# Accumulating DMAs of weight sums moved into the first feed-forward and the second attention, one PSUM copy moved ahead of the GELU, and GpSimd making three of seven low halves there

## The chip, the core and the metric

The kernel is one program on one core of a Trainium2 chip. The metric is the device time of one execution in microseconds (us), as the median of several runs; lower is better. TensorE (PE) multiplies, VectorE (DVE), ScalarE (ACT) and GpSimd (POOL) do the rest, and DMA queues bring weights from device memory (HBM) into SBUF. SyncE (SP) only issues DMAs here. GpSimd issues the DMAs of the sums on a queue of its own.

## The reference, cut to what matters

Two transformer-like blocks run one after the other on 512 positions of width 1024, all in float32:

```python
x = first_block(x, ...)     # stick-breaking attention, pooling and gating branches,
                            # then ff = square(relu(h @ w_ff_in)) @ w_ff_out    (1024 -> 4096 -> 1024)
x = second_block(x, ...)    # differential attention with 256 context rows, a long convolution (by spectra),
                            # then conv_ffn
def conv_ffn(h, p):
    a, b = jnp.split(h @ p["ffn_w_up"], 2, axis=-1)      # 1024 -> 2 x 2816
    a = short_conv(a, p["ffn_conv_w"], p["ffn_conv_b"])  # 3 taps along the positions
    return (jax.nn.gelu(a, approximate=False) * b) @ p["ffn_w_down"]
```

The change touches the weights of `ffn_w_up` in the last line, and times at which they are prepared during the first block's feed-forward and the second block's attention.

## The kernel before, in words

Every float32 product is made of three faster ones: each operand is split into a high and a low half (`wh`, `wl` for weights), and PE adds high by high, low by high and high by low. So each 512 KB unit of weights (128 x 1024) goes through a fixed line of work. SP loads it into one of four `raw` buffers (`load`, L3124) when the low half of the unit four loads earlier has been made. ACT copies it to `wh` (L1356) when PE has used the unit four before it (`SLOTS = 4`). Then `wl = raw - wh` is made by DVE (L2043) or, if the unit is in the list `POOL_LOW`, by GpSimd (L2823). PE takes the units strictly in order, and so do the three others: each engine's program is one list, and `weights(u)` in it means "do your part of all units up to u". In the first feed-forward SP also loads, through the same ring, "mod" halves that DVE reduces (L2029, L2031).

The up-projection of the last feed-forward is cheaper than the plain one for 18 of its 22 column blocks m (m 4 to 11 are run 0, m 12 to 21 are run 1): instead of eight quarter products per m it makes seven, with weight quarters a, b, c, d and their sums ac, cd, acd, abcd. I call it the paired stage. One unit there holds two quarters and is called a duo; there are 63 (28 in run 0, 35 in run 1), each read by PE in 2 x 1.44 us. Seven duos serve two m's: position 0 of the seven holds (d, b), then (ac, abcd), (cd, a), (acd, d), (b, ac), (abcd, cd), (a, acd). For each m PE makes the products abcd(m-1), cd(m), a(m-1), acd(m), d(m), b(m-1), ac(m-1) in this order. Between them ACT and DVE patch partial results in PSUM: ACT copies cd's result aside (`keep_cd`, tile `p1c`, L1940), for which PE waits before d(m); DVE makes `gate_right(m-1)` (L2743, after `value_right`, L2738), for which PE waits before b(m-1) (`times_b`). In the same lists stand the activation of earlier m's: `centre` (ACT L1915), `up_conv` (DVE L2708), `gelu` (ACT L1920), `up_gate` (DVE L2714), `gated_high` (ACT L1926, tile `FFh`) and GpSimd's `FFl` (L3050).

The sums of weights are made in HBM by DMAs from GpSimd's queue (`sum_weights(n, step)`, n the run), 2048 KB each for run 0 and 2560 KB for run 1. Step 0 copies c twice (into ac and cd), step 1 accumulates a and d onto these, step 2 copies ac to acd, step 3 accumulates d, step 4 copies acd to abcd, step 5 accumulates b. Each step's issue waits on GpSimd until the step before has landed (semaphore `d_sum`), and SP's first load of a sum waits for all eight DMAs of its run. GpSimd's queue also loads 12 units whose halves were made ahead ("pre" units, `load_pre`, `wh<-in_wd` and `wl<-in_wd`, L2833 and L2834) and the spectral tables.

Of the kernel before, what the change touches and what calls it, by code (L numbers as in the profile page):

```python
# [165 lines left out]
DUOS = [u for u, (j, _, _) in enumerate(UNITS) if PLAN[j][0] == "sums"]  # L166
# [12 lines left out]
for _n, (_kind, _x, _) in enumerate(LOADS):  # L179
# [9 lines left out]
POOL_LOW = [u for u in range(NU) if u not in PRE and (  # L189
    u < 2 or AT["w_in_2", 0, 1536][0][0] + SLOTS - 1 <= u < AT["w_out_2", 0, 0][0][0] + SLOTS - 1  # L190
    or any(u == AT[x][0][0] for x in (((0, 1, 2), 0, 0), ((1, 1, 2), 0, 0), ("w_ff_in", 0, 0)))
    or u in DUOS and DUOS.index(u) % 7 in (2, 5))]
KT = range(8)


# [97 lines left out]
def program(nc, a):  # L293
    ctx = ExitStack()
    with ctx:
# [185 lines left out]
        def duo_ahead(f, m):  # L481
            return AT[f, m, 0][0][0] + SLOTS - 1
# [859 lines left out]
        def scalar_program(engine):  # L1342
# [176 lines left out]
            for m in range(EARLY, 8):  # L1519
                q = m - EARLY  # L1520
# [421 lines left out]
            def keep_abcd(m):  # L1942
                e.wait_ge(*PART("abcd", m))
                if m > run[0]:
                    e.wait_ge(*ADDED("c", m - 1))
                act(P5C[:, :], PS[:, BANK["up", m, 0], LEFT_HALF], ACT.Copy).then_inc(sem("part_cp"), 1)

            for first_m, count in ((0, 12), (12, 10)):
                run = RUNS[first_m > 0]
                for m in range(first_m, run[0]):  # L1950
                    weights(unit("ffn_w_up_2", 0, 2816 + m * P) + SLOTS - 1)
                    centre(m)
                    gelu(m)
                    gated_high(m, first_m)
                    for i in ((0, 1), (2, 3), (4,), ())[m]:
                        turned_high(i)
                weights(duo_ahead("cd", run[0]))
                keep_cd(run[0])
                weights(duo_ahead("d", run[0]))
                for m in run[1:]:  # L1960
                    weights(duo_ahead("abcd", m - 1))
                    keep_abcd(m - 1)
                    if m - 2 in run:
                        gelu(m - 2)
                    weights(duo_ahead("cd", m))
                    keep_cd(m)
                    if m - 2 in run:
                        gated_high(m - 2, first_m)
                    weights(duo_ahead("a", m - 1))
                    weights(duo_ahead("acd", m))  # L1970
                    weights(duo_ahead("d", m))
                    weights(duo_ahead("b", m - 1))
                    centre(m - 1)
                    weights(duo_ahead("ac", m - 1))
                m = run[-1]
                weights(duo_ahead("abcd", m))
                keep_abcd(m)
                gelu(m - 1)
                gated_high(m - 1, first_m)
                weights(unit("ffn_w_down_2", first_m * P, 0) + SLOTS - 1)  # L1980
                weights(duo_ahead("b", m))
                centre(m)
                gelu(m)
                gated_high(m, first_m)
                if first_m:
                    tables("sqrt_and_others")
                for n in range(2):
                    weights(unit("ffn_w_down_2", (first_m + count - 1) * P, n * S) + SLOTS - 1)
                    for i in range(4 if first_m else 0):
                        q = 4 * n + i  # L1990
                        if q == 7:

                            for c, s in ((0, 7), (1, 12)):
                                cols = slice(256 * c, 256 * c + 256)
                                e.wait_ge("dn_xv", 2 + c)
                                act(T(3)[:, cols], half(X, 3, 1)[:, cols], ACT.Square,
                                    accum_out=NL[:, s:s + 1]).then_inc(sem("dn_sq"), 1)
                            root(NL[:, 19:20], NL[:, 11:12], D, "nl_v", 8).then_inc(sem("nl_rt"), 1)
                            e.wait_ge("nl_v", 9)
                            e.wait_ge("fin_y", 1)  # L2000
                            act(half(Y, 3, 0), half(Y, 3, 0), ACT.Copy, scale=NL[:, 23:24]).then_inc(sem("fin_a"), 1)
                            e.wait_ge("fin_a", 1)
                            engine.dma_start(a["out"][3 * P:4 * P, 0:S], half(Y, 3, 0)).then_inc(sem("d_out"), 16)
                            continue
                        e.wait_ge(*X_READY("dn", q))
                        act(T(q % 4), half(X, i, n), ACT.Square,
                            accum_out=NL[:, 2 * i + n:2 * i + n + 1]).then_inc(sem("dn_sq"), 1)
                        if n:
                            root(NL[:, 16 + i:17 + i], NL[:, 8 + i:9 + i], D, "nl_v", 2 * i + 1).then_inc(sem("nl_rt"), 1)
# [801 lines left out]
        def gpsimd_program(engine):  # L2811
# [155 lines left out]
            for q in range(32):  # L2967
                e.wait_ge("ff_hi", q + 1)
                tt(FFl[:, q % 16, :], T(2 + q % 2), f32(FFh[:, q % 16, :]), ALU.subtract).then_inc(sem("ff_lo"), 1)  # L2969
                if q == 1:  # L2970
                    put_spectrum(0, 1)

            e.wait_ge("p_ff", 32)
            load_tables(1, 0)
            e.wait_ge("w_used", TAIL["w_ff_out"])
            load_tables(1, 1)
            for i in range(0, 8, 4):
# [20 lines left out]
                tt(x, x, T(r % 2), ALU.add).then_inc(sem("rp_add"), 1)  # L2998


            sum_weights(0, 0)
            mine = [u for u in range(PRE[2] + 1) if u > unit("w_in_2", 0, 0) and (u in POOL_LOW or u in PRE)]
            for i, u in enumerate(mine):
                weights(u)
                if i in (0, 3, 5):
                    sum_weights(0, (0, 3, 5).index(i) + 1)
            sum_weights(0, 4)
            for o in range(2):
                for f in range(4):
                    n = 4 * o + f  # L3010
                    if f < 3:
                        weights(unit("dft_f", 128, f * P, o) + SLOTS - 1)
                    for c in range(2):
                        e.wait_ge("ys_hi", 2 * n + c + 1)
                        tt(YS[n % 3][1][:, c, :], T(2 + 2 * (n % 2) + c), f32(YS[n % 3][0][:, c, :]),
                           ALU.subtract).then_inc(sem("ys_lo"), 1)
                    if f >= 2:
                        weights(unit("dft_i", 0, 0, o) + SLOTS - 1 if f == 2 else unit("dft_i", P, 0, o) + SLOTS - 1)
                weights(unit("dft_i", 3 * P, 0, o) + SLOTS - 1)
                e.wait_ge("ac_v", 4 * o + 2)  # L3020
                e.wait_ge("u_ev", 4 if o == 0 else 8)
                tt(U[:, 2, 0:512], T(4), U[:, 2, (o + 1) * S:(o + 2) * S], ALU.mult).then_inc(sem("z_p"), 1)
                if o == 0:
                    weights(unit("w_in_2", 0, 1536 + 9 * P) + SLOTS - 1)
                    weights(unit("w_in_2", 0, 1536 + 10 * P) + SLOTS - 1)
                    sum_weights(0, 5)
            sum_weights(1, 0)


            weights(unit("w_out_2", 3 * P, 0) + SLOTS - 1)  # L3030
            for q in range(6):
# [1 line left out]
                e.wait_ge("o2_v", q + 1)  # L3033
                e.wait_ge("d_xb", 16)
                tt(x, x, T(q % 4), ALU.add).then_inc(sem("o2_xp"), 1)
            sum_weights(1, 1)


            for hf in range(2):
# [23 lines left out]
            for first_m, count in ((0, 12), (12, 10)):  # L3063
                run = RUNS[first_m > 0]
                if first_m == 0:
                    shared_sums()
                    for m in range(run[0]):
                        gated_low(m, 0)
                        if m == 1:
                            sum_weights(1, 2)  # L3070
                weights(duo_ahead("d", run[0]))
                for m in run[1:]:
                    weights(duo_ahead("cd", m))
                    if m - 2 in run:
                        gated_low(m - 2, first_m)
                    weights(duo_ahead("ac", m - 1))
                    if m in (5, 7, 9):
                        sum_weights(1, 3 + (5, 7, 9).index(m))
                gated_low(run[-1] - 1, first_m)
                weights(duo_ahead("b", run[-1]))  # L3080
                gated_low(run[-1], first_m)
                for q in range(6 if first_m else 8):
                    x = half(X, q % 4, q // 4)
                    c = (8 if first_m else 0) + q
                    e.wait_ge("dn_v", c + 1)
                    e.wait_ge("n4_xn", 4)
                    e.wait_ge("o2_xv", 2)
                    e.wait_ge("dn_xp", c - 7)
                    tt(x, x, T((4 if first_m else 0) + q % 4), ALU.add).then_inc(sem("dn_xp"), 1)  # L3089
# [325 lines left out]
```

## Time and profile before

| | |
|---|---|
| median of 3 runs | 1484.92 us (1484.43 to 1485.36) |
| the profiled execution | 1485.86 us, of which the span 1484.1 us |
| mean granted clock of PE | 0.987 of full |
| busy share: PE, DVE, ACT, POOL | 97%, 59%, 44%, 26% |
| DMA | 243 MB, mean 164 GB/s |

The span goes from the first to the last recorded instruction, and all times of rows are measured from its start. Stages in the order of time: first attention to about 330 us, first feed-forward to about 765 us, second block's attention and spectral part to about 1090 us, its feed-forward with the paired stage from about 1140 us (run 0) and 1315 us (run 1). PE is nearly always busy, so the few places at which it waits are what other engines and queues cost.

### The profile page before, as it was taken

What the parts mean: (1) busy time and instruction counts of PE and PEld (TensorE: products, weight loads), DVE (VectorE), ACT (ScalarE), POOL (GpSimd) and SP (SyncE); (2) the same over time, 40 slices, a digit from 0 to 9 for tenths busy, and PEclk for the clock granted to TensorE, in tenths of its full rate; (3) what the DMA queues carried; (4) which work ended last, traced back from release to release, by engine and by line L of the source; (5) the groups of instructions that cost most, each with busy time, mean ns of one, the idle gap of its engine ahead of it and who ended that gap; (6) DMA issues with size and microseconds to landing.
All of it is one profiled execution on the core that took longest, in us unless ns stands there. A gap on an engine that the chain in (4) does not pass through costs nothing.

```text
span 1484.1 us, 19430 instructions
## 1 busy us (share of the span) xinstructions
PE 1439.5 (97%) x7644; PEld 1215.6 (82%) x7644; DVE 876.9 (59%) x1319; ACT 656.9 (44%) x1048; POOL 380.7 (26%) x317
## 2 busy tenths in 40 slices
PE   9999999999999999999999999997999897999998
PEld 7777778888888888888888888886898896889987
DVE  6456665533666543654376367786568575347854
ACT  6545763223544322343363256553445453135542
POOL 1363220111032100220033312154435331133312
PEclk9999999999999999999999999998999898999999
DMA  8351117545265453556345374566785785335541
GB/s 271 113 176 48 58 56 264 170 149 184 85 214 182 143 170 128 173 177 207 128 139 195 129 210 147 151 219 207 276 188 202 218 250 171 110 111 163 173 140 57
DMA packets 72740, 243.15 MB, mean 164 GB/s; under 512 B 8455, under 2 KB 9384, under 8 KB 67658
## 3 DMA queue, kind: packets, MB, share of 16 engines
q1 hardware_dynamic: 61274, 181.22, 36.7%
q0 software_dynamic: 9744, 55.05, 13.2%
q10 hardware_dynamic: 1632, 5.64, 1.0%
q8 instruction: 61, 1.00, 0.3%
q14 instruction: 29, 0.24, 0.0%
HBM read 229.28 MB, written 50.35 MB: 188 GB/s over the span
## 4 chain that ended last, share of the span: by engine, by line
PE 82%; DVE 6%; DMA 5%; ACT 4%; issue 2%; POOL 1%; SPq 0%; ACTq 0%; DVEq 0%; POOLq 0%
PE PS L536 79%; PE PS L549 3%; DMA raw<-sums 2%; ACT wh L1356 2%; DVE TMP L2708 2%; DVE wl L2043 2%; DMA wl<-in_wd 1%; DMA raw<-in_up 1%; POOL wl L2823 1%; DVE TMP L2091 0%; POOL X L3089 0%; ACT th L1934 0%; ACT HTh L1378 0%; ACT p1c L1940 0%; DVE HTl L2059 0%
## 5 line engine op out<-in xcount | busy, mean ns | idle before, releaser
L2043 DVE TENSOR_TENSOR wl<-raw,wh 128x1024 fp32r<-128x1024 f32 x220 | 302.0, 1377 | 314.9 <-ACT wh L1356 314.6
L1356 ACT ACTIVATE wh<-raw 128x1024 fp32r<-128x1024 f32 x255 | 266.9, 1054 | 252.7 <-PE PS L536 223.8
L536 PE MATMUL PS<-HTh,wh 128*128 128x512 f32 (+1 forms) x944 | 347.9, 370 | 3.5 <-POOL wl L2823 2.5
L536 PE MATMUL PS<-HTl,wh 128*128 128x512 f32 (+1 forms) x944 | 345.0, 367 | 0.0
L536 PE MATMUL PS<-HTh,wl 128*128 128x512 f32 (+1 forms) x944 | 340.8, 367 | 0.0
L536 PEld LDWEIGHTS PS<-HTh,wh 128*128 128x128 f32 x944 | 178.6, 189 | 38.6 <-issue 10.9
L536 PEld LDWEIGHTS PS<-HTl,wh 128*128 128x128 f32 x944 | 178.6, 189 | 27.1 <-DVE HTl L2059 0.7
L536 PEld LDWEIGHTS PS<-HTh,wl 128*128 128x128 f32 x944 | 176.4, 189 | 29.4 <-DVE wl L2043 0.2
L536 PE MATMUL PS<-wl,FFh 128*128 128x512 f32 (+1 forms) x442 | 169.9, 384 | 0.0
L536 PE MATMUL PS<-wh,FFh 128*128 128x512 f32 (+1 forms) x442 | 169.9, 384 | 0.0
L536 PE MATMUL PS<-wh,FFl 128*128 128x512 f32 (+1 forms) x442 | 169.8, 384 | 0.0
L2823 POOL TENSOR_TENSOR wl<-raw,wh 128x1024 fp32r<-128x1024 f32 x35 | 88.9, 2543 | 180.8 <-ACT wh L1356 159.9
L536 PE MATMUL PS<-th,wh 128*128 128x256 f32 x360 | 106.5, 296 | 22.0 <-ACT p1c L1940 19.4
L536 PE MATMUL PS<-th,wl 128*128 128x256 f32 x360 | 105.4, 293 | 0.0
L536 PE MATMUL PS<-tl,wh 128*128 128x256 f32 x360 | 105.3, 292 | 0.0
L2969 POOL TENSOR_TENSOR FFl<-TMP,FFh 128x512 fp32r<-128x512 f32 x32 | 43.4, 1357 | 219.5 <-ACT FFh L1591 219.5
L536 PEld LDWEIGHTS PS<-wh,FFl 128*128 128x128 f32 x442 | 83.1, 188 | 16.6
L536 PEld LDWEIGHTS PS<-wl,FFh 128*128 128x128 f32 x442 | 83.1, 188 | 16.3
L536 PEld LDWEIGHTS PS<-wh,FFh 128*128 128x128 f32 x442 | 83.1, 188 | 16.3
L536 PEld LDWEIGHTS PS<-th,wh 128*128 128x128 f32 x360 | 72.6, 202 | 24.0 <-ACT p1c L1940 21.1
L536 PEld LDWEIGHTS PS<-tl,wh 128*128 128x128 f32 x360 | 72.8, 202 | 0.1
L536 PEld LDWEIGHTS PS<-th,wl 128*128 128x128 f32 x360 | 72.6, 202 | 0.0
(359 smaller groups left out, 2344.6 us busy)
## 6 DMA issues: line engine op xcount, KB each, us to landing
raw<-in_ws SPq DMA_DIRECT2D x232, 512.0 KB, 4.2
raw<-sums SPq DMA_DIRECT2D x72, 256.0 KB, 3.5
sums<-in_up POOLq DMA_DIRECT2D x6, 2560.0 KB, 19.4
raw<-in_up SPq DMA_DIRECT2D x54, 256.0 KB, 3.6
sums<-in_up POOLq DMA_DIRECT2D x6, 2048.0 KB, 16.9
sums<-sums POOLq DMA_DIRECT2D x2, 2560.0 KB, 12.7
taps<-TMP SPq DMA_DIRECT2D x16, 256.0 KB, 2.4
tab<-in_spec POOLq DMA_DIRECT2D x8, 512.0 KB, 5.7
```

The source lines that it names most:

```text
L536: return nc.tensor.matmul(out, l, r, start=start, stop=stop, skip_group_check=True)
L549: return nc.tensor.transpose(out, in_, IDENT)
L1356: act(WH[u % SLOTS][:, :n], RAW[i % RAWS][:, :n], ACT.Copy).then_inc(sem("w_hi"), 1)
L2043: tt(WL[k][:, :n], RAW[RAW_AT["unit", u, 0] % RAWS][:, :n], f32(WH[k][:, :n]), ALU.subtract).then_inc(sem("lo_dve"), 1)
L2708: stt(z[:, do], ps[:, di], pp("ffn_conv_w_2", 22 * w + m), z[:, do], ALU.mult, ALU.add).then_inc(sem("uc_v"), 1)
L2823: tt(WL[k][:, :n], RAW[RAW_AT["unit", u, 0] % RAWS][:, :n], f32(WH[k][:, :n]), ALU.subtract).then_inc(sem("lo_pool"), 1)
L2969: tt(FFl[:, q % 16, :], T(2 + q % 2), f32(FFh[:, q % 16, :]), ALU.subtract).then_inc(sem("ff_lo"), 1)
```

## The change

There are three parts. First, all twelve steps of sums move. Run 0's steps 0 to 3 stood in the second block's attention and go to the middle of the first feed-forward's first half (after GpSimd's piece q = 15, where GpSimd has no other work for 89 us), steps 4 and 5 into its second half. Run 1's steps stood between the second block's out-projection and the paired stage of run 0; step 0 goes to where run 0's step 0 was, 1 to 4 between the units of the attention, and 5 to the end of the spectral part. No step is left in the paired stage. Second, ACT's `keep_cd(m)` goes ahead of `gelu(m-2)`. Third, GpSimd makes the low halves at positions 1, 3 and 5 of each seven duos, where it made those at 2 and 5, but none in the first four duos of each run.

```diff
@@ POOL_LOW @@
-    or u in DUOS and DUOS.index(u) % 7 in (2, 5))]
+    or u in DUOS and DUOS.index(u) % 7 in (1, 3, 5) and u not in DUOS[:4] + DUOS[28:32])]
@@ scalar_program @@
                     keep_abcd(m - 1)
+                    weights(duo_ahead("cd", m))
+                    keep_cd(m)
                     if m - 2 in run:
                         gelu(m - 2)
-                    weights(duo_ahead("cd", m))
-                    keep_cd(m)
@@ gpsimd_program @@
                 if q == 1:
                     put_spectrum(0, 1)
+                if q == 15:
+                    for step in range(4):
+                        sum_weights(0, step)
 
             e.wait_ge("p_ff", 32)
             load_tables(1, 0)
+            sum_weights(0, 4)
+            sum_weights(0, 5)
             e.wait_ge("w_used", TAIL["w_ff_out"])
             load_tables(1, 1)
...
-            sum_weights(0, 0)
+            sum_weights(1, 0)
             mine = [u for u in range(PRE[2] + 1) if u > unit("w_in_2", 0, 0) and (u in POOL_LOW or u in PRE)]
             for i, u in enumerate(mine):
                 weights(u)
-                if i in (0, 3, 5):
-                    sum_weights(0, (0, 3, 5).index(i) + 1)
-            sum_weights(0, 4)
+                if i in (0, 3, 4, 6):
+                    sum_weights(1, (0, 3, 4, 6).index(i) + 1)
...
                     weights(unit("w_in_2", 0, 1536 + 10 * P) + SLOTS - 1)
-                    sum_weights(0, 5)
-            sum_weights(1, 0)
+            sum_weights(1, 5)
...
                 tt(x, x, T(q % 4), ALU.add).then_inc(sem("o2_xp"), 1)
-            sum_weights(1, 1)
...
                         gated_low(m, 0)
-                        if m == 1:
-                            sum_weights(1, 2)
...
                     weights(duo_ahead("ac", m - 1))
-                    if m in (5, 7, 9):
-                        sum_weights(1, 3 + (5, 7, 9).index(m))
```

GpSimd's list in the first feed-forward (`FFl` is the low half of the activation, made from `FFh`; `sums<-in_up` is a copy or an accumulation):

```order
-L2969 TENSOR_TENSOR FFl_79<-TMP_145,FFh_78 128x512 x30
+L2969 TENSOR_TENSOR FFl_79<-TMP_145,FFh_78 128x512 x14
+L2844 DMA sums<-in_up 256x2048 x2
+L2846 DMA sums<-in_up 256x2048
+L2847 DMA sums<-in_up 256x2048
+L2849 DMA sums<-sums 256x2048
+L2851 DMA sums<-in_up 256x2048
+L2969 TENSOR_TENSOR FFl_79<-TMP_145,FFh_78 128x512 x16
```

Six DMAs now stand between the two halves of the `FFl` pieces, with GpSimd's waits for three landings among them.

DVE's list in the paired stage, one group of seven duos (`wl` are low halves; the removed ones go to GpSimd, the added one comes from it):

```order
-L2043 TENSOR_TENSOR wl_76<-raw_68,wh_72 128x1024
 L2732 TENSOR_TENSOR PS<-PS,p1c_140 128x256
 L2714 TENSOR_TENSOR TMP_145<-TMP_145,PS 128x512
+L2043 TENSOR_TENSOR wl_77<-raw_69,wh_73 128x1024
 L2738 TENSOR_TENSOR PS<-PS,p1c_140 128x256
 L2743 TENSOR_TENSOR PS<-p5c_141,PS 128x256
 L2724 TENSOR_TENSOR p1c_139<-PS,p1c_139 128x256
-L2043 TENSOR_TENSOR wl_74<-raw_66,wh_70 128x1024
 L2043 TENSOR_TENSOR wl_75<-raw_67,wh_71 128x1024
```

DVE loses the low halves of positions 1 and 3 and gains that of position 2, and the gained one stands between `up_gate` (L2714) and `value_right` and `gate_right` (L2738, L2743).

ACT's list in the paired stage, the same place:

```order
-L1920 ACTIVATE TMP_145<-TMP_145 128x512
 L1940 ACTIVATE p1c_139<-PS 128x256
-L1926 ACTIVATE FFh_78<-TMP_145 128x512
-L1356 ACTIVATE wh_73<-raw_69 128x1024
-L1356 ACTIVATE wh_70<-raw_66 128x1024
...
+L1920 ACTIVATE TMP_145<-TMP_145 128x512
+L1926 ACTIVATE FFh_78<-TMP_145 128x512
+L1356 ACTIVATE wh_73<-raw_69 128x1024
+L1356 ACTIVATE wh_70<-raw_66 128x1024
```

The copy `p1c` (L1940) is now ahead of the GELU (L1920). `wh_73`, the high half for position 2, stays behind `FFh` (L1926).

## Rows read from the trace of the kernel before

**Rows 1.** The page: the chain of waits by line.

```profile
PE PS L536 79%; PE PS L549 3%; DMA raw<-sums 2%; ACT wh L1356 2%; DVE TMP L2708 2%; DVE wl L2043 2%; DMA wl<-in_wd 1%; DMA raw<-in_up 1%; POOL wl L2823 1%; DVE TMP L2091 0%; POOL X L3089 0%; ACT th L1934 0%; ACT HTh L1378 0%; ACT p1c L1940 0%; DVE HTl L2059 0%
```

**Rows 2.** Timeline of PE: start, us, instruction, [idle before it <-what ended it].

```profile
1032.30 0.80 PE L536 MATMUL PS<-EDh,wh 128*128 128x512 f32 x1 [8.92 <-DMA wl<-in_wd]
...
1146.91 0.39 PE L536 MATMUL PS<-th,wh 128*128 128x256 f32 x1 [2.92 <-ACT p1c L1940]
...
1177.17 0.39 PE L536 MATMUL PS<-th,wh 128*128 128x256 f32 x1 [2.61 <-DVE wl L2043]
...
1183.12 0.58 PE L536 MATMUL PS<-th,wh 128*128 128x256 f32 x1 [3.87 <-ACT p1c L1940]
...
1207.59 0.39 PE L536 MATMUL PS<-th,wh 128*128 128x256 f32 x1 [1.69 <-ACT p1c L1940]
...
1236.91 0.58 PE L536 MATMUL PS<-th,wh 128*128 128x256 f32 x1 [8.91 <-ACT p1c L1940]
...
1323.53 0.36 PE L536 MATMUL PS<-HTh,wh 128*128 128x256 f32 x1 [2.50 <-POOL wl L2823]
...
1370.94 0.38 PE L536 MATMUL PS<-th,wh 128*128 128x256 f32 x1 [0.59 <-ACT p1c L1940]
```

**Rows 3.** Windows: length, busy us of PE, PEld, DVE, ACT, POOL, then PEclk, DMA, GB/s.

```profile
1032.00:1038.00 6.00, 5.70 (x13) 4.51 (x14) 0.17 (x1) 1.06 (x1) 0.00 (x0) 0.50 0.33 122
...
1183.00:1187.00 4.00, 3.88 (x18) 3.88 (x19) 2.48 (x3) 2.17 (x4) 4.00 (x2) 0.50 0.11 20
...
1236.00:1242.00 6.00, 5.09 (x24) 5.09 (x25) 3.99 (x6) 3.39 (x5) 4.61 (x2) 0.50 0.27 84
1324.00:1328.00 4.00, 4.00 (x25) 4.00 (x24) 0.18 (x1) 1.43 (x2) 2.37 (x1) 0.63 0.84 255
```

**Rows 4.** The chain in order of time, its waits for DMAs: issue, us to landing.

```profile
1010.96 21.30 DMA wl<-in_wd
...
1157.34 17.44 DMA raw<-in_up
...
1213.46 16.72 DMA raw<-sums
```

**Rows 5.** Timeline of POOL: the issues of sums near these waits.

```profile
1009.83 0.98 POOL L2855 DMA_DIRECT2D sums<-in_up  x1
...
1211.92 0.90 POOL L2855 DMA_DIRECT2D sums<-in_up  x1
```

**Rows 6.** DMA from 1103 to 1113 us: packets, MB, share of 16 engines.

```profile
q0 software_dynamic: 202, 1.65, 82.3%
q1 hardware_dynamic: 203, 0.77, 20.6%
```

**Rows 7.** Timeline of POOL at the start of run 1.

```profile
1314.06 6.04 POOL L3089 TENSOR_TENSOR X<-X,TMP 128x512 f32<-128x512 f32 x4 [26.59 <-DVE TMP L2798]
```

**Rows 8.** Timeline of DVE, then ACT, then PE in one period of run 1.

```profile
1353.43 1.98 DVE L2043 TENSOR_TENSOR wl<-raw,wh 128x1024 fp32r<-128x1024 f32 x1
...
1357.78 1.22 DVE L2043 TENSOR_TENSOR wl<-raw,wh 128x1024 fp32r<-128x1024 f32 x1
...
1360.31 0.43 DVE L2743 TENSOR_TENSOR PS<-p5c,PS 128x256 f32<-128x256 f32 x1
...
1359.96 0.63 ACT L1926 ACTIVATE FFh<-TMP 128x512 fp32r<-128x512 f32 x1 [1.16 <-DVE TMP L2714]
1360.50 1.99 ACT L1356 ACTIVATE wh<-raw 128x1024 fp32r<-128x1024 f32 x2
...
1361.55 0.28 PE L536 MATMUL PS<-th,wh 128*128 128x256 f32 x1
```

**Rows 9.** DMA from 504 to 593 us: the loads, KB each, median us to landing.

```profile
raw<-in_ws SPq DMA_DIRECT2D x25, 512.0 KB, 4.1
```

**Rows 10.** DMA from 869 to 872 us: the pair of accumulations of run 0.

```profile
sums<-in_up POOLq DMA_DIRECT2D x2, 2048.0 KB, 23.0
```

**Rows 11.** Timeline of ACT, a unit in the first feed-forward.

```profile
526.60 1.06 ACT L1356 ACTIVATE wh<-raw 128x1024 fp32r<-128x1024 f32 x1 [4.38 <-PE PS L536]
```

## The prediction

> **What bounds the kernel now.** I read the page first. PE is busy for 97% of the span, and the chain of waits runs through its matmuls [rows 1]; what is left on it are loads (raw<-sums 2%, wl<-in_wd 1%, raw<-in_up 1%) and pieces of ACT, DVE and GpSimd. So the time is PE's work plus the moments at which PE stands still, and I listed these in PE's timeline [rows 2]: 8.92 us at 1032, 2.92 at 1147, four waits of 2.61, 3.87, 1.69 and 8.91 in run 0, 2.50 at the start of run 1, and in run 1 a small one for `p1c` in each period of 21 us (the row of 0.59 stands for four: 0.22, 0.59, 0.59 and 0.60). Then I read the granted clock behind them, since PE runs on at half its clock after a long wait (level 1.2 instead of 2.4 GHz): 0.50 over the 6 us behind the wait at 1032, over 4 us behind the one at 1183, over 6 us from 1236, and 0.63 over 4 us from 1324 [rows 3]. The shortest wait behind which these rows show a fall is the one of 2.50.
>
> Third, why PE waits. The chain names the transfers: wl<-in_wd 21.30 us from issue to landing, raw<-in_up 17.44, raw<-sums 16.72 [rows 4]. GpSimd's timeline shows a sum issued just before: at 1009.83, a us ahead of the slow wl<-in_wd, and at 1211.92, 1.5 us ahead of the slow raw<-sums [rows 5]. While a sum accumulates, both queues move as many packets (202 and 203 in 10 us) but the sum 1.65 MB and the raw loads 0.77 MB [rows 6]: a load stream gets 77 GB/s, 6.8 us for 512 KB. The late raw holds ACT, and ACT's list holds `p1c`, which is why the rows name `p1c`.
>
> **The change part by part.** Work is neither added nor removed: the same twelve DMAs, the same low halves, the same copies. Only places move.
>
> A. Step 5 of run 0 leaves the spectral part before the pre units. The wait of 8.92 goes, and the half clock behind it, half of 6 us: 3.0. Gain 11.9. Run 1's step 5 comes about 40 us later in GpSimd's list, behind the last pre unit, where the pair of copies of run 1 stood; nothing of weights is late there in the trace before. The earlier steps of run 1 are a quarter larger than run 0's at the same places, where PE had no wait longer than 0.1 us, so I cost them at nothing; without the cover that unit loads have there, a sum of 19 us would cost what step 5 did.
>
> B. No sum runs during run 0. The four waits go, 17.1 us, and the half clock, 3.0 behind 1236 and 2.5 behind 1183 (over 2.0, which the window alone shows). Gain 22.6.
>
> C. The first low half on GpSimd in run 1 goes to DVE. GpSimd is in the additions to X for 6.04 us until 1320.1 before it begins [rows 7], and the wait of 2.50 follows; DVE's list has it before its share of the same out-projection. With the clock (0.37 of 4 us, 1.5) gain 4.0. The same edit in run 0 puts a low half of 1.22 us before `up_gate(3)` on DVE, ahead of the wait of 2.92: I take a loss of 0.5, between 0 and 1.2.
>
> D. `p1c` before the GELU. ACT no longer waits for DVE's `up_conv` before it copies, so the small waits go, 0.59 three times and 0.22: gain 2.0.
>
> E. Three of seven. Fewer low halves on DVE would relieve it, but DVE is not what PE waits for in this stage. What counts is where the added one stands. The order shows `wl_77` (position 2) between `up_gate` and `value_right`, `gate_right`, and PE waits for `gate_right` before b. In the period from 1350 [rows 8]: `gate_right` ran 1360.31 to 1360.74, PE began b at 1361.55, 0.8 us of slack. Now DVE first needs `wh` of position 2, which ACT makes behind `FFh`: `FFh` ended at 1360.5. The removed low half (1357.78, 1.22 us) lets `up_gate` and so `FFh` come earlier by 0 to 1.2 us; I take 0.6. Then wh is ready about 1360.9 (each of the two copies takes 1.0), the low half takes 1.22 alone and 1.98 beside a GpSimd operation; I take 1.3, as `FFl` is nearly over by then: 1362.2. `value_right` and `gate_right` together 0.9: 1363.1, against 1361.55. PE waits 1.5 us, where before it did not; the bounds are 0.8 (1.2 earlier, 1.22) and 2.8 (0 earlier, 1.98). It occurs once in each group of seven, except the first of each run: 3 times in run 0, 4 in run 1, 7 x 1.5 = 10.5 loss, bounds 6 and 20. This is shorter than the waits behind which the clock fell, so I add nothing for it.
>
> The rows show that GpSimd slows a DVE low half (1.22 to 1.98 us). The Trainium skill says the same of the two engines in "GPSIMD Engine Reference", section "1. Specifications": they share access to SBUF and contend when instructions have two SBUF inputs. By that rule three GpSimd lows instead of two would cost DVE up to 0.8 us once more per group, on an engine that is busy for 59%; it changes the sum only where it lengthens the low half in E.
>
> F. Steps 0 to 3 of run 0 under the first feed-forward, from 504 us. There are 25 loads in 89 us [rows 9], one per 3.56 us. Under accumulation a load takes 6.8. The pair took 23.0 us each at the median [rows 10], I take 28 until the second lands: 4.1 loads done instead of 7.9, 13.5 us short. The single one, 16 us: 2.4 instead of 4.5, 7.6 short. The copies let about as much through as is wanted; I take 3 us. Together 24 us late. The cover: `wh` is made every 4.38 + 1.06 = 5.44 us, each time when PE frees a slot [rows 11], so a low half is ready 3 x 5.44 less 2.3 = 14 us before PE needs it. A raw is asked for four loads ahead: 14.2 us at the mean interval, 21.8 where all four are units; less 2.3 and the 4.1 of the load 8 to 15 us. Cover 22 to 29 against 24: thin, yet two of the terms come from stretches in which loads had to wait for nothing else. The mod halves of the ring can be late without any loss. I take 0, and 3 to 12 us if it does not hold. GpSimd is back at about 504 + 13 + 28 + 11 + 16 = 572 (the other steps' times by the same view as [rows 10]), before 593. Steps 4 and 5 meet a lighter stretch: nothing.
>
> The rule behind the packet counts stands in the Trainium skill, "DMA: Bandwidth & Descriptors", section "Queues, rings and completion order": a DMA engine alternates between its rings packet by packet. The trace agrees (202 to 203). It speaks against this move, since larger packets of the sums take the larger part wherever they run; that is rival 2.
>
> Sum: 11.9 + 22.6 + 4.0 + 2.0 - 0.5 - 10.5 = 29.5 us off the span of 1484.1: 1454.6. The profiled execution took 1485.86, 1.8 more than its span, and the median of the runs is 1484.92, 0.8 more than the span. On that scale: 1455.4, rounded to 1455.
>
> **The rivals.**
> 1. The new wait for `gate_right` does not come, or is under 0.3 us, because PE is itself later or `FFh` earlier than I take it. For it: 0.8 us of slack today. Against it: the order of DVE's list and `wh` behind `FFh`. Time: the sum without the 10.5, 1445, or 1447 with 0.3 in each group. Chance 0.22.
> 2. The first feed-forward starves: PE waits 3 to 12 us about 545 to 590, with some 2 us of half clock. For it: the cover of F is no larger than the lateness at its lower bound. Time 1458 to 1468. Chance 0.25.
> 3. Run 0's waits stay in part, being ACT's list and not the DMAs: 1207.59 and 1177.17 remain and grow. Against it: run 1, with the same lists and no sum, has only 0.59. Time 1465 to 1475. Chance 0.04.
> 4. Slower than before: the feed-forward starves for good, since GpSimd, waiting for landings, is not back for `FFl` at 593 and the loads run at a still lower share. This decides from 30 us of waiting in the first feed-forward, thus when loads get under half of the 77 GB/s. Nothing in the rows is near that. Time 1487 to 1500. Chance 0.02.
> The forecast itself (E there, F hidden) has 0.45, with a range of its own of 1450 to 1460; 0.02 is left for what I do not see.
>
> **How the numbers follow.** The range takes the forecast's bounds (E 6 to 20: 1450 to 1465), most of rival 1 above 1443 and the smaller half of rival 2: 1443 to 1466 holds about 0.45 + 0.18 + 0.19 = 0.82. A measurement of this kernel tells about 0.2% (3 us) from no change. Faster by more: all but rival 4 and half of what is left, 0.96; same 0.01; slower 0.03.
>
> **What would show it.** At about 1010 to 1030 wl<-in_wd lands within 7 us and PE has no wait at the place of 1032. In run 0 PE has none over 3 us behind its start, raw loads take 3 to 5 us. In the paired stage PE's waits name DVE L2743, about 1.5 us each, seven of them, and none names `p1c` in run 1. At the start of run 1 no POOL wl. In the feed-forward from 504 raw loads take 8 to 16 us and ACT's wh waits for raw, but PE does not. The prediction is wrong if PE waits for wh or wl between 540 and 593, if L2743 never ends a wait of PE, or if sums of 2560 KB in the attention hold up a unit there.

## The result and the profile after

The changed kernel takes 1459.37 us at the median of four runs (1456.29 to 1461.92), against 1484.79 us for the kernel before (1484.43 to 1485.36, four runs): a ratio of 0.9828, 95% interval 0.9804 to 0.9851, so 25.4 us faster. The prediction was 1455 (1443 to 1466). The profiled execution took 1457.4 us with a span of 1455.7 us, 28.4 us less than the span before; the forecast span was 1454.6.

The page of the changed kernel: busy time by engine, then the chain of waits by line, which answers to [rows 1].

```profile
PE 1429.8 (98%) x7644; PEld 1206.5 (83%) x7644; DVE 855.4 (59%) x1314; ACT 657.1 (45%) x1048; POOL 386.1 (27%) x322
...
PE PS L536 83%; DMA raw<-in_ws 3%; PE PS L549 3%; DVE wl L2043 2%; ACT wh L1356 1%; DVE TMP L2708 1%; DVE TMP L2714 1%; DVE TMP L2091 0%; ACT th L1934 0%; ACT TMP L1920 0%; DVE PS L2743 0%; ACT HTh L1378 0%; DVE HTl L2059 0%; DVE tl L2718 0%; ACT p1c L1940 0%
```

The loads raw<-sums, wl<-in_wd and raw<-in_up have left the chain, and raw<-in_ws, the ordinary weight loads, have come onto it. The timeline of PE shows where it still stands; these rows answer to [rows 2].

```profile
569.90 0.50 PE L536 MATMUL PS<-wh,FFh 128*128 128x512 f32 x1 [0.59 <-DVE wl L2043]
...
587.92 0.47 PE L536 MATMUL PS<-HTh,wh 128*128 128x512 f32 x1 [1.41 <-DVE wl L2043]
...
1137.25 0.58 PE L536 MATMUL PS<-th,wh 128*128 128x256 f32 x1 [3.28 <-ACT p1c L1940]
...
1159.99 0.38 PE L536 MATMUL PS<-th,wh 128*128 128x256 f32 x1 [1.33 <-DVE PS L2743]
...
1375.88 0.39 PE L536 MATMUL PS<-th,wh 128*128 128x256 f32 x1 [1.32 <-DVE PS L2743]
```

The last two rows are the first and the last of seven (1160.0, 1181.7, 1203.5, 1310.7, 1332.4, 1354.2, 1375.9). Nothing is left at the place of 1032, none of the four waits of run 0, none at the start of run 1, and none for `p1c` but the one at the start of run 0. New are the seven waits for `gate_right` and two in the first feed-forward. The waits of PE that differ add up to 33.4 us before (8.92, 2.92, 2.61, 3.87, 1.69, 8.91, 2.50 and 2.00 for `p1c` in run 1) and 14.6 us after (0.59, 1.41, 3.28 and 9.3): 18.8 of the 28.4 us. The rest is the clock. In windows of 2 us, PE's busy time times the part of the clock that was missing adds up to about 12.6 us before (3.0 behind 1032, 7.9 in run 0, 1.7 behind 1324) and 2.8 us after. Two of the windows after (they answer to [rows 3]):

```profile
1137.00:1143.00 6.00, 5.75 (x27) 5.75 (x28) 3.22 (x3) 1.48 (x3) 0.57 (x1) 0.52 0.65 194
1159.00:1163.00 4.00, 3.01 (x25) 3.02 (x26) 1.22 (x4) 1.28 (x2) 2.36 (x1) 1.00 0.50 162
```

Only the wait of 3.28 us is followed by the lower level (0.52 over 6 us). Behind 1.33 us of waiting the granted clock stayed at 1.00, and so it did behind the two waits of the first feed-forward. Before, [rows 3] show four such stretches, and a fifth lay behind 1147 (0.57 over 4 us).

Why PE waits for `gate_right` is seen in one period, first DVE, then ACT, then PE; it answers to [rows 8].

```profile
1349.47 0.69 DVE L2714 TENSOR_TENSOR TMP<-TMP,PS 128x512 f32<-128x512 f32 x1 [1.12 <-ACT TMP L1920]
1351.81 1.48 DVE L2043 TENSOR_TENSOR wl<-raw,wh 128x1024 fp32r<-128x1024 f32 x1 [1.65 <-ACT wh L1356]
1353.21 0.42 DVE L2738 TENSOR_TENSOR PS<-PS,p1c 128x256 f32<-128x256 f32 x1
1353.66 0.43 DVE L2743 TENSOR_TENSOR PS<-p5c,PS 128x256 f32<-128x256 f32 x1
...
1350.20 0.63 ACT L1926 ACTIVATE FFh<-TMP 128x512 fp32r<-128x512 f32 x1 [0.75 <-DVE TMP L2714]
1350.73 1.99 ACT L1356 ACTIVATE wh<-raw 128x1024 fp32r<-128x1024 f32 x2
...
1354.15 0.38 PE L536 MATMUL PS<-th,wh 128*128 128x256 f32 x1 [1.33 <-DVE PS L2743]
```

DVE ends `up_gate` at 1350.2 and stands idle for 1.65 us, since its next work is the low half of position 2 and ACT makes that high half only behind `FFh`. Then come the low half (1.48), `value_right` and `gate_right`, and PE goes on when the last is done.

### The profile page after: what moved, and what is told of

The parts are those of the page before. It is cut to its first block, busy times and chain, and to the rows that moved or that the text cites. A ratio compares the mean times of both kernels' runs of the same rounds, so it can differ in the third digit from the quotient of the medians.

```text
span 1455.7 us, 19430 instructions
## 1 busy us (share of the span) xinstructions
PE 1429.8 (98%) x7644; PEld 1206.5 (83%) x7644; DVE 855.4 (59%) x1314; ACT 657.1 (45%) x1048; POOL 386.1 (27%) x322
## 4 chain that ended last, share of the span: by engine, by line
PE 86%; DVE 6%; ACT 3%; DMA 3%; issue 1%; POOL 0%; ACTq 0%; DVEq 0%; POOLq 0%
PE PS L536 83%; DMA raw<-in_ws 3%; PE PS L549 3%; DVE wl L2043 2%; ACT wh L1356 1%; DVE TMP L2708 1%; DVE TMP L2714 1%; DVE TMP L2091 0%; ACT th L1934 0%; ACT TMP L1920 0%; DVE PS L2743 0%; ACT HTh L1378 0%; DVE HTl L2059 0%; DVE tl L2718 0%; ACT p1c L1940 0%
## 5 line engine op out<-in xcount | busy, mean ns | idle before, releaser
L2043 DVE TENSOR_TENSOR wl<-raw,wh 128x1024 fp32r<-128x1024 f32 x215 | 280.5, 1309 | 325.9 <-ACT wh L1356 325.6
L2823 POOL TENSOR_TENSOR wl<-raw,wh 128x1024 fp32r<-128x1024 f32 x40 | 101.3, 2536 | 191.3 <-ACT wh L1356 170.4
L536 PE MATMUL PS<-th,wh 128*128 128x256 f32 x360 | 103.3, 287 | 12.6 <-DVE PS L2743 9.3
L536 PE MATMUL PS<-th,wl 128*128 128x256 f32 x360 | 102.4, 284 | 0.0
L536 PEld LDWEIGHTS PS<-th,wh 128*128 128x128 f32 x360 | 69.5, 193 | 14.3 <-DVE PS L2743 10.7
L536 PEld LDWEIGHTS PS<-tl,wh 128*128 128x128 f32 x360 | 69.6, 193 | 0.1
L536 PEld LDWEIGHTS PS<-th,wl 128*128 128x128 f32 x360 | 69.6, 193 | 0.0
```

What stands on the lines that cost most here:

```text
L536: return nc.tensor.matmul(out, l, r, start=start, stop=stop, skip_group_check=True)
L2043: tt(WL[k][:, :n], RAW[RAW_AT["unit", u, 0] % RAWS][:, :n], f32(WH[k][:, :n]), ALU.subtract).then_inc(sem("lo_dve"), 1)
L2823: tt(WL[k][:, :n], RAW[RAW_AT["unit", u, 0] % RAWS][:, :n], f32(WH[k][:, :n]), ALU.subtract).then_inc(sem("lo_pool"), 1)
```

## The experiments

Ten kernels ran, in three batches on two chips, each batch beside its own runs of the kernel before (medians 1483.70, 1484.65 and 1484.35 us); the changed kernel's own runs are those of the section on the result. I compare ratios; 0.001 of a ratio is 1.5 us. All of them keep the whole computation.

| kernel | median us (range) | ratio to before, 95% interval |
|---|---|---|
| changed kernel | 1459.37 (1456.29 to 1461.92) | 0.9828, 0.9804 to 0.9851 |
| e1: changed, `gate_right` first | 1448.15 (1442.18 to 1449.29) | 0.9751, 0.9733 to 0.9770 |
| e2: changed, positions 2 and 5 | 1451.40 (1447.40 to 1456.06) | 0.9782, 0.9762 to 0.9801 |
| e3: before, sums moved | 1456.01 (1452.22 to 1458.29) | 0.9810, 0.9794 to 0.9825 |
| e4: before, positions 1, 3, 5 | 1485.24 (1483.95 to 1486.40) | 1.0008, 0.9999 to 1.0017 |
| e5: before, copy ahead of GELU | 1473.75 (1471.78 to 1475.65) | 0.9929, 0.9917 to 0.9942 |
| e6: changed, run 0's sums in the first attention | 1454.35 (1453.16 to 1454.69) | 0.9800, 0.9786 to 0.9813 |
| e7: e6 and e1 | 1443.49 (1442.04 to 1444.32) | 0.9723, 0.9710 to 0.9737 |
| e8: e6, positions 2 and 5 but for one duo | 1443.27 (1442.65 to 1444.27) | 0.9722, 0.9708 to 0.9735 |
| e9: before, step 5 of run 0 later | 1477.14 (1474.79 to 1478.32) | 0.9950, 0.9937 to 0.9962 |
| e10: changed, sums in shorter packets | 1454.71 (1453.82 to 1455.29) | 0.9798, 0.9784 to 0.9812 |

### e1: is it the place of the low half in DVE's list?

```diff
-                    weights(duo_ahead("cd", m))
-                    weights(duo_ahead("a", m - 1))
                     value_right(m - 1)
                     gate_right(m - 1)
+                    weights(duo_ahead("cd", m))
+                    weights(duo_ahead("a", m - 1))
```

> The changed kernel with one edit in DVE's list: value_right and gate_right ahead of the low halves of weights(cd, m) and weights(a, m-1). Theory: the seven waits of 1.33 us for DVE L2743 come from the low half of position 2 standing ahead of gate_right, so they go and the time falls by about 9 us against the changed kernel (1459 to about 1450, or 1447 where the first feed-forward is as in the profiled run). Rival: DVE is short of time in this stage, so the wait only moves to a low half (PE waits for DVE wl L2043 or L2724's product) and the time stays within 3 us of the changed kernel.

Measured: 0.9751 against 0.9828, about 11 us faster than the changed kernel, where I expected 9. In PE's timeline all seven waits for L2743 are gone and no wait over 0.3 us has come in their place; behind the start of run 0 PE does not wait at all. The theory holds, the rival (DVE short of time) falls. Why it is 11 us and not 9 is said under E below. The first feed-forward was worse in the profiled run of this kernel than in the changed one's, where that part of the program is the same. Its timeline of PE there:

```profile
554.48 0.50 PE L536 MATMUL PS<-wh,FFh 128*128 128x512 f32 x1 [1.33 <-DVE wl L2043]
...
568.34 0.75 PE L536 MATMUL PS<-wh,FFh 128*128 128x512 f32 x1 [2.68 <-DVE wl L2043]
...
773.62 0.47 PE L536 MATMUL PS<-wh,tab 128*128 128x512 f32 x1 [0.37 <-issue]
```

and the window behind the second wait:

```profile
568.00:574.00 6.00, 5.67 (x18) 4.56 (x19) 2.65 (x4) 1.06 (x1) 0.00 (x0) 0.72 1.04 236
```

The matmul that the third row shows, the first with the spectral tables, is a marker behind the first feed-forward: it began at 767.8 in the kernel before, 769.8 in the changed one, here at 773.6. So this stage cost 2.0 us in the one and 5.8 in the other, and the clock went down with the wait of 2.68 (0.72 over 6 us).

### e2: GpSimd's positions as before

```diff
-    or u in DUOS and DUOS.index(u) % 7 in (1, 3, 5) and u not in DUOS[:4] + DUOS[28:32])]
+    or u in DUOS and DUOS.index(u) % 7 in (2, 5))]
```

> The changed kernel with GpSimd's positions as before the change (2 and 5, with no exception for the first four duos). Theory: the seven waits for L2743 go (9.3 us), the wait for GpSimd's low half at the start of run 1 comes back with its slow clock (2.5 + 1.5 us), run 0 starts 0.4 us sooner: about 5 us faster than the changed kernel, 1454. Rival: three of seven relieves DVE and is worth something, so that this is not faster than the changed kernel.

Measured: 0.9782 against 0.9828, 7 us faster than the changed kernel, with intervals that do not overlap. The profile has no wait for L2743, and the one at the start of run 1 is back (2.51 us for POOL wl L2823), as is the 2.93 instead of 3.28 us at the start of run 0. The theory's rows are all there. The first feed-forward has waits of 2.78 and 0.74 us, and the marker stands at 771.84. Three of seven is a loss in the changed kernel as its list of DVE stands.

### e3: the sums alone

The edit is the gpsimd part of the change's diff, made to the kernel before.

> The kernel before with only the sums moved as in the change (positions 2 and 5, GELU ahead of the copy). Theory: the sums alone carry the gain: 34.5 us of waits and slow clock less 2 to 5 us in the first feed-forward, so 1452 to 1456, as fast as or faster than the whole change. Rival: part of run 0's waits came from ACT's list, so it is 5 us or more slower than the theory says and PE still waits for p1c in run 0 by more than 1 us a period.

Measured: 0.9810, 28 us faster than before, the whole gain of the change and 2.7 us more at the median (the intervals overlap). In run 0 PE waits for `p1c` by 0.22, 0.60 and 0.63 us, as in run 1. The first feed-forward, with the same sums in it, has no wait over 0.3 us in this profiled run, and the marker stands at 767.60. So the sums carry the change.

### e4 and e5: the two other parts alone

e4 is the change's line of `POOL_LOW` in the kernel before.

> The kernel before with only GpSimd's positions changed (1, 3 and 5, none in the first four duos of a run). Theory: this part costs by itself: up to seven waits of about 1.3 us for DVE L2743 (those of run 0 may hide in its waits for sums), less 4.0 us for the wait at 1323 and its slow clock: 0 to 5 us slower than the kernel before. Rival: three of seven is worth something by itself, the time falls by 4 us or more.

Measured: 1.0008, no difference that the runs can tell. PE waits for DVE L2743 once in run 0 and three times in run 1 (1.52 to 1.54 us each; two more are under 0.3 us), two long waits of run 0 are shorter (7.42 for 8.91, 2.94 for 3.87), and the wait of 2.50 at the start of run 1 is gone. The forecast of 0 to 5 us slower holds at its lower end.

e5 has the change's edit of ACT's list alone.

> The kernel before with only the copy p1c ahead of the GELU. Theory: the four waits of 0.22 to 0.60 us in run 1 go, 2.0 us, and run 0's long waits stay, since raw loads come late there: 1 to 3 us faster than before. Rival: run 0's waits come from the GELU ahead of the copy, so that 1183 and 1236 go too, 15 us or more.

Measured: 0.9929, 10.5 us faster, where I expected 1 to 3. That theory falls in its number. The timeline of PE in run 0, to be held against [rows 2]:

```profile
1175.84 0.39 PE L536 MATMUL PS<-th,wh 128*128 128x256 f32 x1 [1.56 <-DVE wl L2043]
...
1182.10 0.39 PE L536 MATMUL PS<-th,wh 128*128 128x256 f32 x1 [2.72 <-DVE PS L2743]
...
1204.96 0.47 PE L536 MATMUL PS<-th,wh 128*128 128x256 f32 x1 [2.46 <-DVE PS L2743]
...
1226.11 0.39 PE L536 MATMUL PS<-th,wh 128*128 128x256 f32 x1 [2.12 <-DVE wl L2043]
...
1232.37 0.57 PE L536 MATMUL PS<-th,wh 128*128 128x256 f32 x1 [2.72 <-DVE PS L2743]
```

and the windows behind two of them:

```profile
1182.00:1186.00 4.00, 3.90 (x32) 3.91 (x33) 3.16 (x5) 3.12 (x4) 1.82 (x2) 1.00 0.71 228
...
1232.00:1238.00 6.00, 5.63 (x34) 5.63 (x35) 4.97 (x9) 3.63 (x5) 1.29 (x1) 0.72 0.52 175
```

The raw loads are nearly as late as before (ACT waits 7.42 and 7.99 us for them, before 8.84 and 8.59), but the waits add up to 11.6 instead of 17.1 us, and the clock stays up behind 1182 (1.00 against 0.50) and is 0.72 instead of 0.50 behind 1232. It is lower in one place: 0.57 over the 4 us from 1205, where it was 1.00 behind 1207 before. In windows of 2 us the missing clock of run 0 adds up to 4.6 us against 7.9. So there are 5.5 us of waiting, 2.0 us in run 1 and 3.3 us of clock, 10.8 against the 10.2 between the profiled spans (1484.1 and 1473.9). A late load of run 0 had cost twice: once as itself, and again because ACT, late by it, still waited for DVE's `up_conv` ahead of the copy for which PE waited. ACT's timeline in the kernel before:

```profile
1181.22 0.63 ACT L1920 ACTIVATE TMP<-TMP 128x512 f32<-128x512 f32 x1 [3.48 <-DVE TMP L2708]
```

Rival 3 of the prediction has this much truth in it.

The parts do not add: 28 and 10.5 alone, less 1 for the positions, against 25.4 together. Two things make up the 12 us. The copy's new place was good for late loads that moving the sums takes away: of its 10.5 us about 4 are left (25.4, and 7 more that e2 gives back, less 28). And the positions cost 7 us where PE has no other waits (e2), but 1 in the kernel before, where they shorten the long waits of run 0.

### e9: is step 5 the cause of the wait at 1032?

```diff
                     weights(unit("w_in_2", 0, 1536 + 10 * P) + SLOTS - 1)
-                    sum_weights(0, 5)
+            sum_weights(0, 5)
             sum_weights(1, 0)
```

> The kernel before with run 0's step 5 alone behind the last pre unit of the spectral part, just ahead of run 1's step 0. Theory: wl<-in_wd lands within 7 us, PE's wait of 8.92 us at 1032 and the slow clock behind it go, 11 to 12 us faster than before, with run 0's waits where they were. Rival: the wait at 1032 is DVE's and ACT's chain to ysl and only shows a late transfer, so less than 4 us is won.

Measured: 0.9950, 7.5 us faster; the profiled span is 11.0 us shorter (1473.1). The wait of 8.92 us is gone with its slow clock, which refutes the rival. Run 0's waits are there as expected, of other sizes (3.68 at its start, then 1.30, 4.25, 1.78 and 7.74 us). The timeline of PE shows a new one behind the new place, where the pair of copies of run 1 now follows step 5:

```profile
1065.06 0.50 PE L536 MATMUL PS<-wh,O3h 128*128 128x512 f32 x1 [2.57 <-DVE wl L2043]
```

DVE's low half ahead of it took 5.17 us, where in the kernels before and after it takes 2.25 and 2.24 beside the same additions of GpSimd (X, L3035), and these two have no wait over 0.3 us there. GpSimd's first four additions took 5.03 us here against 6.05 there, and the low half ended 1.1 us behind the last of them: GpSimd went through at its own pace and DVE gave way, where in the other two kernels both were slowed. What decides between the two stays open. That the medians show 3.5 us less than the profiles is a matter of which run was profiled: this one is the fastest of its five, 2.4 us below their median, and the one of the kernel before (1485.86) lies 1.2 us above the median here.

### e6: run 0's sums where the queues are idle

```diff
+            sum_weights(0, 0)
             keep_scores(0)
...
                 if p + 2 < PAIRS:
                     keep_scores(p + 2)
+                if p in (0, 5, 8, 11):
+                    sum_weights(0, 1 + (0, 5, 8, 11).index(p))
...
                 tt(BC[m][:, S:], EG[3 * m + 1], EG[3 * m + 2], ALU.add).then_inc(sem("eg_add"), 1)
+            sum_weights(0, 5)
...
-                if q == 15:
-                    for step in range(4):
-                        sum_weights(0, step)
...
-            sum_weights(0, 4)
-            sum_weights(0, 5)
```

> The changed kernel with run 0's six steps in the first attention (from 117 us, where the DMA engines are busy for 17%) and none in the first feed-forward. Theory: the two waits of PE at 570 and 588 (0.59 and 1.41 us in the profiled run) and the spread of the changed kernel's runs (1456 to 1462) come from raw loads under the sums of the first feed-forward; both go, 2 us against the profiled run and 2 to 5 against the median, about 1455, runs within 1 us of each other. Rival: the spread has another source, then the runs still differ by 4 to 5 us and the median falls by at most 2 us.

Measured: 0.9800 against 0.9828, 4 us faster than the changed kernel (the intervals overlap by 0.0009), and the runs lie within 1.5 us of each other instead of 5.6. The marker is back at 767.62, and no wait over 0.3 us stands in the first feed-forward; of its sum issues on GpSimd only steps 4 and 5 waited, 5.1 us each, in a place where GpSimd has nothing urgent. The two waits came from the sums under the feed-forward, and with them, as far as four runs of each can tell, the spread.

### e10: by packets?

```diff
-max_dma_last_dim=8192
+max_dma_last_dim=4096
```

(in all seven lines of `sum_weights` that start a DMA)

> The changed kernel with the sums' DMAs cut at half the length (max_dma_last_dim 4096 instead of 8192). Theory: queues alternate by packets, so packets of 4 KB on both sides give raw loads half of the rate instead of a third: loads under accumulation take 4 to 5.5 us each, PE's waits in the first feed-forward shrink below 1 us, the runs differ less, and the sums take a quarter or more longer: 1 to 4 us faster than the changed kernel. Rival: the share is not by packets (or the accumulation itself is the limit), so raw loads stay as slow, the sums only take longer, and the time stays or rises.

The views of DMA while the pair of accumulations runs, 538 to 553 us, in the changed kernel:

```profile
q0 software_dynamic: 328, 2.52, 80.7%
q1 hardware_dynamic: 335, 1.22, 21.8%
```

and the same stretch with shorter packets:

```profile
q0 software_dynamic: 537, 2.13, 71.1%
q1 hardware_dynamic: 512, 1.90, 33.8%
```

In both the two queues move nearly the same number of packets; with packets half as long the raw loads get 1.90 MB instead of 1.22 in 15 us (127 against 81 GB/s). The pair of accumulations takes GpSimd's wait from 29.8 to 32.4 us, and no wait of PE over 0.3 us is left in the first feed-forward. The time is 0.9798, 4.5 us faster than the changed kernel (the intervals overlap by 0.0008), with runs within 1.5 us, just as when the sums are elsewhere. The theory holds but for the price: the accumulations took 9% longer, not a quarter or more. By the rule of the Trainium skill that the prediction weighed ("DMA: Bandwidth & Descriptors", "Queues, rings and completion order") this is what alternation by packets would give, and the counts of both kernels agree with it.

### e7 and e8: both cures together

e7 is e6 with e1's edit. e8 is e6 with this line:

```diff
+    or u in DUOS and DUOS.index(u) % 7 in (2, 5) and u != DUOS[30])]
```

> The changed kernel with both edits that helped it: run 0's sums in the first attention and gate_right ahead of the low halves in DVE's list. Theory: they add, 1454.35 less 9.3 us: 1445, with runs within 1.5 us of each other, PE's only wait over 0.5 us in the paired stage being the one of 3.3 us at the start of run 0. Rival: one edit hides the other's gain, 1448 or more.

> The changed kernel with run 0's sums in the first attention, and GpSimd at positions 2 and 5 as before the change, but for the one duo at the start of run 1. Theory: the seven waits for L2743 go, the wait of GpSimd at the start of run 1 stays away, the first wait of run 0 is 2.9 instead of 3.3 us: 1444 to 1445, the same as or up to 1 us faster than three of seven with gate_right first. Rival: three of seven relieves DVE, so this is 2 us or more slower than that kernel.

Measured: 0.9723 and 0.9722, 1443.5 and 1443.3 us, 41 us below the kernel before and 16 below the changed one. In the paired stage of e8 the timeline of PE has one row left over 0.3 us (e7 has the same row with 3.28):

```profile
1134.93 0.58 PE L536 MATMUL PS<-th,wh 128*128 128x256 f32 x1 [2.93 <-ACT p1c L1940]
```

The edits add. Two or three of seven on GpSimd makes no difference once PE does not wait for `gate_right`: DVE is not the bound here.

## Why the prediction was right, and where its sizes were off

The number alone could not have told: 1459.4 lies in the range of rival 2 (1458 to 1468) as well. The terms can.

**A, step 5 of run 0 (11.9 us).** Right. e9 gave 11.0 between the profiles and 7.5 between the medians, with a small new wait at its own place. In the changed kernel the `wh` and `wl` loads of the pre units issued between 1005 and 1030 us land in 6.0 and 6.7 us at the median, before in 13.8 and 14.5, and PE has no wait there. The larger steps of run 1 in the attention cost nothing, as forecast.

**B, run 0 (22.6 us).** Right in size: e3 and the changed kernel have none of the long waits. Only half right in its cause. I put all of it down to late loads; e5 shows that these cost 17.1 us of waiting only with the GELU ahead of the copy, and 11.6 without. Since the change takes away both, the sum was not hurt, but D's 2.0 us was no measure of what that edit can do alone.

**C, start of run 1 (4.0 us).** Right: the wait is gone in the changed kernel and back in e2.

**The start of run 0 (loss of 0.5).** Right for the wait, which grew from 2.92 to 3.28 us. The clock behind it is 0.52 over 6 us, where the trace before shows it at 0.57 over 4 us behind 1147. That is about 1.2 us more, so 1.5 us between the two profiles. But the 1.2 us is not the change's: the same wait of 3.3 us is followed by 0.72 over 6 us in e6 and 0.51 in e7, and the one of 2.93 by 0.72 in e2 and 0.52 in e8. The prediction had left the slow clock behind 1147 out.

**D, the small waits (2.0 us).** Right, they are gone.

**E, the new wait (loss of 10.5, seven of 1.5 us).** Right in kind, place and number; the rows show 1.33 us each, 9.3 us. The rows understate it. From one such wait to the next are 21.73 us in e6, and one period without the wait is 20.16 us in e7: 1.57 us in each group of seven, 11.0 in all, which is what e1 and e7 gained. PE's matmuls start every 0.12 us and are recorded with 0.28 each, so the idle time is counted from 1352.82, though the last start was at 1352.54; the next is at 1354.15. ACT began on the high halves 2.1 us before PE wanted b (1350.73 against 1352.82), where I reckoned 1.65; the low half then took 1.48 us instead of 1.3. e1 and e2 show the cause from both sides. Rival 1 falls.

**F, sums under the first feed-forward (0).** This is the term that failed. PE waits for `wl` at 569.9 and 587.9, which the prediction had named as a sign that it was wrong, and rival 2 (waits of 3 to 12 us, 0.25) came in part. The four profiled runs with the same program in this stage have 2.0 us of waiting (the changed kernel), 4.0 (e1), 3.5 (e2) and none over 0.3 (e3). The view of DMA from 506 to 521 us, during the pair of copies:

```profile
q0 software_dynamic: 497, 3.93, 69.4%
q1 hardware_dynamic: 384, 1.41, 30.9%
...
raw<-in_ws SPq DMA_DIRECT2D x3, 512.0 KB, 11.9
```

That is 94 GB/s for raw loads, 5.6 us for each where 3.56 are wanted, and the pair took 20.9 us from issue to the next step, not 13. So "the copies let about as much through as is wanted" is wrong for the pair. But the two places at which PE waited lie later. ACT's timeline there, first in the kernel before, then in the changed one (the same units; this trace runs 0.5 us ahead of the other up to the sums, as at 526.60 and 526.11):

```profile
553.80 1.06 ACT L1356 ACTIVATE wh<-raw 128x1024 fp32r<-128x1024 f32 x1 [4.38 <-PE PS L536]
...
570.12 1.06 ACT L1356 ACTIVATE wh<-raw 128x1024 fp32r<-128x1024 f32 x1 [4.38 <-PE PS L536]
```

```profile
549.48 1.06 ACT L1356 ACTIVATE wh<-raw 128x1024 fp32r<-128x1024 f32 x1 [16.87 <-DMA raw<-in_ws]
...
567.52 1.06 ACT L1356 ACTIVATE wh<-raw 128x1024 fp32r<-128x1024 f32 x1 [5.52 <-DMA raw<-in_ws]
...
585.46 1.06 ACT L1356 ACTIVATE wh<-raw 128x1024 fp32r<-128x1024 f32 x1 [14.10 <-DMA raw<-in_ws]
```

The high half is 4.1 us late at 519 and on time again at 526.11. Under the pair of accumulations (31 us from issue to the next step, where I had 28, with 81 GB/s for the loads) it falls behind, to 14.2 us at 567.52. It gains on this while the single copy runs (2.31 MB of loads in 12.4 us, 2.8 us for each) and is 6.1 us late at 570.29; the last accumulation brings it to 15.8 us at 585.46. So there are two peaks, and the prediction had added up the shortfalls of all the steps to one of 24 us, as if nothing were made good between them.

The cover was too large as well. PE waited by what the high half was late beyond 13.6 to 13.9 us, in all six waits of the changed kernel, e1 and e2 (peaks of 14.2 to 17.9 us); with 12.0 us in e3 and 7.1 in e10 there was no wait. The 14 us for made halves was thus right. The 8 to 15 us on top, for raws asked for ahead, were not there: the load behind the row of 549.48 landed about 17 us later than before, and the high half was 12.5 us later, so 4 to 5 us were covered. The two errors worked against each other, and that the term came within some us of 0 is luck.

With the measured terms the sum is 11.9 + 22.6 + 4.0 + 2.0 - 1.5 - 9.3 - 2.0 = 27.7, against 28.4 between the profiled spans (the waits as the rows show them, on both sides). The median lies 4 us above the forecast, and e6, without F, at 1454.35: the 4 us are F, which differs from run to run. In the prediction's numbers themselves, rival 2's waits and clock on the forecast of 1455.4 give 1460 to 1469, not 1458 to 1468, and the 0.19 of its 0.25 that the range takes is more than "the smaller half".

## What to carry to other kernels

When work is shifted from one engine to another in a kernel with fixed lists, the gained engine time is of less interest than what now stands ahead of the item the bounding engine waits for: look for the input of each moved item, and who is queued behind it. A large background transfer should be priced in bytes per turn of the queues (its packets against the loads' packets) over its whole chain, copies too, and placed where the DMA engines are idle, or cut into packets as short as those of the loads it runs beside. Its lateness is followed step by step against the cover, with what is made good between the steps, not added up. A late input can cost twice where the list has a second, unrelated wait ahead of the item that the bounding engine waits for (5.5 us of waiting in e5), so that item goes first.

## What was not expected of the hardware

Queues share by packets closely enough that halving the packets of one raised the other's rate by more than half (81 to 127 GB/s), while the accumulations took only 9% longer (a wait of 32.4 for 29.8 us).

The length of PE's wait did not tell by itself whether the granted clock fell. It was 0.57 over 4 us behind 2.46 us (e5, 1205) and 0.72 over 6 us behind 2.68 us (e1, 568), but 1.00 behind 2.57 us (e9, 1065), 2.72 us (e5, 1182) and 2.78 us (e2, 567).

And the same program varied by 5.6 to 8.7 us where the loads beside the sums come late enough to hold up PE in some runs (the changed kernel, e1, e2, e3), and by 1.5 to 2.3 us where they do not (e6, e7, e8, e10: 1.5, 2.3, 1.6 and 1.5), with four or five runs of each.
